# Two transformer blocks on one core: another order of projection items and of hosted weights, and TensorE products that nobody reads in the norms

## The reference, cut to what matters

```python
def first_block(x, c, ...):
    for l in range(2):
        sh1, sc1, g1, sh2, sc2, g2 = split(silu(c) @ w_ada[l] + b_ada[l])
        h = x * (1 + sc1) + sh1
        y = mixer(h)                       # h @ w_in, attention, @ w_o
        x = layer_norm(ALPHA * x + (1 + g1) * y)
        h = x * (1 + sc2) + sh2
        x = layer_norm(ALPHA * x + (1 + g2) * swiglu(h, w_ffn_in[l], w_ffn_out[l]))

def second_block(x, c, ctx, c_ctx, ...):
    for l in range(2):
        mod_x, mod_c = ada_params(c, w_ada[l]), ada_params(c_ctx, w_ada[l])   # 9 vectors each
        x, h_ctx = swiglu_half_step(x, mod_x), swiglu_half_step(h_ctx, mod_c)
        p = modulate(rms_norm(x)) @ w_in[l]          # q, k, v; rms norm and rotation per head
        x = x + gate * (attention(p) @ w_out[l])
        x, h_ctx = swiglu_half_step(x, mod_x), swiglu_half_step(h_ctx, mod_c)
```

## Time and profile before

| | |
|---|---|
| median of 3 runs | 2866.78 us (2857.04 to 2866.90) |
| profiled execution | 2865.56 us, its span 2863.7 us |
| mean granted TensorE clock | 0.937 |
| busy: TensorE, VectorE, ScalarE, GpSimd | 2611.6, 1771.5, 1083.2, 226.9 us |
| DMA | 413.74 MB, mean 144 GB/s |

### The profile page before, as it was taken

The page is one execution under the profiler, slowest core; times in us unless marked ns, Lnnn a source line. Parts: engine busy times, 40 slices in busy tenths (PEclk is TensorE's granted clock), DMA queues, the critical chain, the costliest instruction groups (busy, mean ns, idle before and its releaser), DMA issues.

```text
span 2863.7 us, 39671 instructions
## 1 busy us (share of the span) xinstructions
PE 2611.6 (91%) x15379; PEld 2228.5 (78%) x15379; DVE 1771.5 (62%) x3184; ACT 1083.2 (38%) x2068; POOL 226.9 (8%) x170
## 2 busy tenths in 40 slices
PE   4767998897997899998999899999899998999999
PEld 4746997867997688887875678888688887877899
DVE  6567776658776656546559675555565433568654
ACT  2343543444443333323338333322333322336553
POOL 2000100000100211101000021110111100100110
PEclk8868999979999999998899999999999999789999
DMA  8923775814765244332520334433344433441553
GB/s 291 279 96 118 265 247 165 263 50 148 240 224 184 78 143 133 131 125 90 152 74 2 118 103 144 135 125 114 100 147 132 133 121 128 105 128 61 178 186 122
DMA packets 354869, 413.74 MB, mean 144 GB/s; under 512 B 24737, under 2 KB 291914, under 8 KB 354618
## 3 DMA queue, kind: packets, MB, share of 16 engines
q1 hardware_dynamic: 352496, 404.13, 44.2%
q0 software_dynamic: 832, 4.65, 0.5%
q10 hardware_dynamic: 1354, 2.43, 0.2%
HBM read 409.56 MB, written 5.27 MB: 145 GB/s over the span
## 4 chain that ended last, share of the span: by engine, by line
PE 62%; DVE 9%; ACT 2%; DMA 2%; issue 1%; POOL 0%; DVEq 0%; ACTq 0%; POOLq 0%
PE bank L894 61%; DVE ada_partial L1533 2%; DMA raw_weights<-in_w_ffn_in_dram 2%; DVE H_hi L1660 1%; DVE weight_lo L682 1%; PE bank L1146 1%; DVE tmp L1643 1%; DVE rstd L1633 1%; ACT weight_hi L1230 1%; DVE X L1648 0%; DVE rstd L1755 0%; DVE bias L1759 0%; DVE X L1715 0%; POOL H_lo L852 0%; DVE bank L1795 0%
## 5 line engine op out<-in xcount | busy, mean ns | idle before, releaser
L682 DVE TENSOR_TENSOR weight_lo<-raw_weights,weight_hi 128x512 fp32r<-128x512 f32 x1024 | 776.1, 765 | 915.9 <-ACT weight_hi L1230 905.1
L1230 ACT ACTIVATE weight_hi<-raw_weights 128x512 fp32r<-128x512 f32 x1024 | 634.1, 629 | 1355.5 <-PE bank L894 1226.1
L894 PE MATMUL bank<-H_hi,weight_hi 128*128 128x256 f32 (+1 forms) x2832 | 973.7, 344 | 109.4 <-POOL H_lo L852 79.9
L894 PE MATMUL bank<-H_lo,weight_hi 128*128 128x256 f32 (+1 forms) x2832 | 955.0, 337 | 0.0
L894 PE MATMUL bank<-H_hi,weight_lo 128*128 128x256 f32 (+1 forms) x2832 | 953.9, 337 | 0.0
L894 PEld LDWEIGHTS bank<-H_hi,weight_hi 128*128 128x128 f32 x2832 | 554.4, 196 | 192.3 <-issue 119.2
L894 PEld LDWEIGHTS bank<-H_hi,weight_lo 128*128 128x128 f32 x2832 | 554.5, 196 | 52.0
L894 PEld LDWEIGHTS bank<-H_lo,weight_hi 128*128 128x128 f32 x2832 | 555.2, 196 | 49.0 <-issue 1.0
L1533 DVE SCALAR_TENSOR_TENSOR ada_partial<-raw_weights,silu_c,ada_partial 128x512 f32<-128x512 f32 x616 | 441.6, 744 | 1.6 <-issue 0.4
L894 PE MATMUL bank<-hidden_hi,weight_hi 128*128 128x256 f32 (+1 forms) x1056 | 358.3, 339 | 3.2 <-DVE weight_lo L682 3.2
L894 PE MATMUL bank<-hidden_hi,weight_lo 128*128 128x256 f32 (+1 forms) x1056 | 354.9, 336 | 0.0
(11 more groups left out here) (170 smaller groups left out, 2050.1 us busy)
## 6 DMA issues: line engine op xcount, KB each, us to landing
raw_weights<-in_w_ada_dram SPq DMA_DIRECT2D x120, 1024.0 KB, 5.3
raw_weights<-in_w_ffn_up_dram SPq DMA_DIRECT2D x88, 1024.0 KB, 5.3
raw_weights<-in_w_ffn_in_dram SPq DMA_DIRECT2D x44, 1024.0 KB, 6.0
raw_weights<-in_w_ffn_down_dram SPq DMA_DIRECT2D x32, 1024.0 KB, 5.1
raw_weights<-in_w_in_dram SPq DMA_DIRECT2D x18, 1024.0 KB, 6.0
raw_weights<-in_w_ffn_out_dram SPq DMA_DIRECT2D x16, 1024.0 KB, 7.7
raw_weights<-in_w_in_ab_dram SPq DMA_DIRECT2D x12, 1024.0 KB, 9.8
raw_weights<-in_w_in_cd_dram SPq DMA_DIRECT2D x12, 1024.0 KB, 8.7
```

Of the source, the lines that this page charges most:

```text
L682: eng.tensor_tensor(WL[:, p.g % SPLIT, 0:p.kt * CW].rearrange("p (t n) -> p t n", n=CW), raw_ap(ch.n, ch.kt, CW)[:, p.k0:p.k0 + p.kt, :], ...
L894: return pe.matmul(o, w, x, start=start, stop=stop, skip_group_check=True)
L1230: act.activation(WH[:, p.g % SPLIT, 0:p.kt * CW].rearrange("p (t n) -> p t n", n=CW), raw_ap(ch.n, ch.kt, CW)[:, p.k0:p.k0 + p.kt, :], ACT ...
```

## The change

- In layers 2 and 3 the `k 0` item comes before `kv`; the first round of the norm per head is renamed to match.
- The projection of layer 0 hosts 10 chunks instead of 12, that of layer 2 five instead of four, that of layer 3 two instead of four. The last `ffn_in`, which had no host, hosts what is left (three chunks, in its first three steps); the tests for a host are now made per step.
- TensorE gets `busy(n)`: n fp32 products of `ident` with `ones` into a PSUM bank that the stage does not use otherwise; nobody reads them. An `rms` norm has 6 before its wait for X and 22 behind its last sum; an `ln` norm 4 before, 4 behind the sums of X, one behind each square product, and 12 at the end.
- VectorE's steps of `ffn_in` are written out by one call; their order is the same.

```diff
-    ROUNDS = ((12, 8, 9), (10, 11, 4, 5), (6, 7, 0, 1), (2, 3))
+    ROUNDS = ((8, 9, 12), (10, 11, 4, 5), (6, 7, 0, 1), (2, 3))
...
-            a1 = ada_chunk() if host else None
+            a1 = ada_chunk() if host and len(ADA) < sum(ADA_CHUNKS) else None
...
+        done = len(ADA) if steps[-1].host is None and host else None
+        add("ffn_in", hosted=done, n=n, steps=steps, ...
...
-            groups.append(Rows(chunks=cs, host=ada_chunk() if host and m < 3 else None,
+            groups.append(Rows(chunks=cs, host=ada_chunk() if steps[-1].host and m < 3 else None,
...
-        all_hosted = len(ADA) if len(ADA) == sum(ADA_CHUNKS) else None
+        all_hosted = len(ADA) if ada == 3 else None
...
-         (2816, ("v", 768))], T, 12, T, 0)
+         (2816, ("v", 768))], T, 10, T, 0)
...
-            [(2048, ("kv",)), (1024, ("k", 0)), (1280, ("k", 2)), ...
-             (256, ("q", 2)), (1536, ("v", 0)), (1792, ("v", 256))], n, 4, T if last else n, 2 + l)
+            [(1024, ("k", 0)), (2048, ("kv",)), (1280, ("k", 2)), ...
+             (256, ("q", 2)), (1536, ("v", 0)), (1792, ("v", 256))], n, 2 if last else 5, T if last else n, 2 + l)
...
-        ffn(a["w_ffn_up_2"][l, 1], a["w_ffn_down_2"][l, 1], n2, 2 + l, 8, True, not last, False)
+        ffn(a["w_ffn_up_2"][l, 1], a["w_ffn_down_2"][l, 1], n2, 2 + l, 8, True, True, False)
...
+        def busy(n):
+            for _ in range(n):
+                mm(B_T[1][:, 0:P], ident[:, :], ones[:, :], True, True)
+
         def stats(s, before):
+            busy(6 if s.kind == "rms" else 4)
             pe.wait_ge(x_ready.sem, s.x)
             for m in range(3 if before.kind == "proj" else 0, 4):
                 sums(s, m)
             if s.kind == "ln":
+                busy(4)
                 for t in range(NT):
                     squares(s, t, B_T[0])
+                    busy(1)
+            busy(22 if s.kind == "rms" else 12)
...
+            if s.hosted:
+                close(s.hosted)
```

More of the change, by code:

```diff
@@ L519, in ffn @@
             g = chunk("g", view(w_in), 0, KC, CW * s)
-            a1 = ada_chunk() if host else None
+            a1 = ada_chunk() if host and len(ADA) < sum(ADA_CHUNKS) else None
             u = chunk("g", view(w_in), 0, KC, DFF + CW * s)
             steps.append(Step(g=g, u=u, host=a1, gg=group("act"), ug=group("dve")))
-        add("ffn_in", n=n, steps=steps, silu=silu_g.take(11), a32=act32.take(11), hi=act_hi.take(11),
+        done = len(ADA) if steps[-1].host is None and host else None
+        add("ffn_in", hosted=done, n=n, steps=steps, silu=silu_g.take(11), a32=act32.take(11), hi=act_hi.take(11),
             ready=act_ready.take(11), host=host)
@@ L641, in _build @@
         qkv(a["w_in_2"][l],
-            [(2048, ("kv",)), (1024, ("k", 0)), (1280, ("k", 2)), (512, ("q", 4)), (768, ("q", 6)), (0, ("q", 0)),
-             (256, ("q", 2)), (1536, ("v", 0)), (1792, ("v", 256))], n, 4, T if last else n, 2 + l)
+            [(1024, ("k", 0)), (2048, ("kv",)), (1280, ("k", 2)), (512, ("q", 4)), (768, ("q", 6)), (0, ("q", 0)),
+             (256, ("q", 2)), (1536, ("v", 0)), (1792, ("v", 256))], n, 2 if last else 5, T if last else n, 2 + l)
         add("bias", what="na", layer=l, take=bias_in.take(16 * 34))
@@ L742, in step @@
                 load(at, lambda k: s.steps[k].g)
-                if s.host:
+                if s.steps[at.u].host:
                     load(at, lambda k: s.steps[k].host)
@@ L1669, in step @@
             def step(at):
-                ahead_of(at, lambda k: s.steps[k].g, (lambda k: s.steps[k].host) if s.host else None)
+                ahead_of(at, lambda k: s.steps[k].g, (lambda k: s.steps[k].host) if s.steps[at.u].host else None)
                 ahead_of(at, lambda k: s.steps[k].u)
@@ L1681, in step @@
                 dve.sem_inc(ev_dve.sem, 1)
[L1682 to L1688, removed]
+            each(dve, 0, 11, 2, step)
+            if s.hosted:
+                close(s.hosted)
         def proj(s):
```

## The result

The changed kernel took 2820.7 us (median of four, 2814.8 to 2827.6) where the one before took 2865.5: ratio 0.9846, 95% interval 0.9821 to 0.9871. That is 44.8 us less. Run again beside other kernels (`after_again`) it took 2823.9 us (six, 2817.6 to 2838.8), ratio 0.9861 (0.9834 to 0.9887). The profiled execution is the longest of the first four: 2827.6 us, span 2825.8, which is 37.9 us under the span before. So the traces can account for 37.9 us; the other 7 are in how the changed kernel's executions differ among themselves, and they differ with the clock (0.964 at 2814.8 us, 0.963 and 0.962 at 2819.6 and 2821.9, 0.959 at 2827.6).

What follows compares the result with a forecast made beforehand. TensorE was taken as the bound, by its own stream, its stops and slices at half clock. Terms -12.1 - 10.6 - 6.3 - 2.6 + 1.9 - 4 = -33.7 us took 2865.6 to 2832 us; range 2822 to 2856.

Steps and rivals of the forecast that it cites:

- Part 1, layer 2: Layer 2 projection: with `k 0` before `kv`, first product to the item behind takes 35.8 us, not 47.9; 12.1 us less.
- The fifth host, put at 0: Layer 2 projection: a fifth hosted item, 8 more partial products on VectorE, hidden behind TensorE; 0, at worst 2 us.
- Part 1, layer 3: Layer 3 projection: the same reordering takes 35.0 us, not 45.6; 10.6 us less.
- the term put at 0: Layer 3 projection: losing two hosts changes nothing, since they hid behind TensorE; 0 us.
- Part 2: Layer 0 projection: two hosts fewer let scores start about 154.9 instead of 161.16; -6.3 us, bounds 0 and -7.
- Part 3: Moved hosted chunks: layer 1's first two feed-forward steps 12.2 us each, -2.6 us; two sums in the last feed-forward, +1.9 us.
- Part 4: Norms: unread products at 0.23 us each lie mostly in waits and warm the statistics; together -4.3, taken as -4 us.
- The one that I gave 0.21: Rival: `kv` falls back in layer 2 alone, behind its 16-instruction sum; -12.1 becomes about +2, 2846 us; chance 0.21.
- Unread products costing on the path: Rival: in the norms they cost +3.4 in each of four layer norms; 2852 us at most, 2845 middle; chance 0.09.
- both `kv` cold: Rival: `kv` is cold wherever it stands, layers 2 and 3 pay +4 and +5 instead of gaining; 2863 us; chance 0.12.
- the slower case: Rival: the clock counts neither fp32 unread nor narrow products; `kv` cold twice, unread ones cold too; 2883 us; chance 0.03.

Runs made afterwards that it cites:

- b_order: The kernel before with only `k 0` put ahead of `kv`, hosts as before and no unread products: 2841.2 us, ratio 0.9912.
- b_unread: The kernel before with only the unread products added, in all ten norms; `kv` first and hosts as before: 2859.0 us, ratio 0.9969.
- b_hosts: The kernel before with only the hosted chunks moved as in the change; `kv` first, no unread products: 2854.0 us, ratio 0.9947.
- a_no_unread: The changed kernel without its unread products, all else as changed: 2843.1 us, ratio 0.9916.
- a_shift9: The changed kernel with nine more unread products (2.1 us) between the halves of layer 2's first feed-forward: 2842.2 us, ratio 0.9907.
- a_shift4: The changed kernel with four more unread products (0.9 us) between the halves of layer 2's first feed-forward: 2828.5 us, ratio 0.9849.

## Why the prediction was off, point by point

**Part 1, layer 2: right.** `k 0` to its last tile is 15.04 us (15.06), the sum 1.70 (1.71), `kv` 16.35 instead of 17.5: a tile is 2.04, the narrow products (2.04 - 3 x 0.25)/12 = 0.108 apart, just beyond the lower bound of 0.11, and the 32-bit loads of the ada sum were a good guide. From the first product to the item behind, 1365.38 - 1330.80 = 34.6, so 13.3 less instead of 12.1. The Trainium skill (TensorE: Matmul & The Clock Gate, Back-to-back issue gap) gives about 81 ns for a 128-column product with its load, and an estimate from that had `kv` at 13.8 us; the trace, with 16.35, does not agree. The fifth host, put at 0, costs its sum: from there to the first scores 102.70 us after 101.15 (1490.66 - 1389.51, the first scores before), 1.6 more.

**Part 1, layer 3: the size was off.** -10.6 was forecast; from the first product to the first scores it is 2526.10 - 2413.15 = 112.95 after 128.74 (2565.66 - 2436.92), 15.8 less. The item pair gave 11.9, a sum that no longer stands on the path 0.8, and 3.1 came from what I had not costed: TensorE waits 1.99 us for a reciprocal in both kernels; before, the clock was at 0.53 for the 10.94 us behind that wait, after at 0.78 for 7.83 us with the same work. Part of this goes with the hosts that layer 3 lost, which I had put at 0. The same work behind that wait, over the same 45 or 46 products, in the kernel before, in `b_order` and `b_unread`, which have layer 3's four hosts as well, and in `b_hosts`, which has two:
```profile
2514.66:2526.03 11.37, 11.37 (x45) 8.76 (x46) 4.57 (x8) 1.44 (x3) 0.00 (x0) 0.55 0.63 200
2487.31:2497.11 9.80, 9.80 (x45) 7.93 (x46) 4.57 (x8) 1.43 (x3) 0.00 (x0) 0.65 0.75 237
2509.03:2517.36 8.33, 8.33 (x46) 6.42 (x46) 4.57 (x8) 1.44 (x3) 0.00 (x0) 0.80 0.89 279
2507.07:2513.88 6.81, 6.81 (x46) 5.34 (x46) 4.56 (x8) 1.44 (x3) 0.00 (x0) 1.00 0.49 156
```
So with four hosts it takes 8.3 to 11.4 us in three profiles; the fourteen with two show 6.8 us (eight of them) or 8.3 (six, the changed kernel among them). From the norm's reciprocal to attention `b_hosts` takes 133.8 us after 141.3, and `a_no_unread` 123.6 after `b_order`'s 128.3. By these pairs of single profiles, and the changed kernel's 125.1, the term put at 0 is worth 3 to 7.5 us, sums included, and it accounts for what `b_hosts` gave beyond the 7 expected. Why the clock is higher behind that wait with two hosts fewer, no run shows.

**Part 2: right.** Scores start at 154.59 (forecast 154.9), -6.6 us for the -6.3.

**Part 3.** The last feed-forward is 1.5 longer (1.9). Layer 1's stage gave less than 2.6: ada sums two steps apart come 26.0 and 26.5 us apart where they were 26.8 and 27.0, so 1.3 in all; its first item takes 0.7 of that back (13.77 us at 0.55 after 13.11 at 0.86). A step is still VectorE's, at 13.0 us and not 12.2.

**Part 4: this step failed.** I took the unread products at -4, counting the cover and the faster sums of squares, and nothing for what they do to the clock of the stages behind them. The local terms came out: 0.23 us each, over 2.76 us before the first tile, squares of `rms` no longer cold (-1.6 once, though `b_hosts` has the same 786.4 us without any unread product), 8 squares of a layer norm with their unread products in 5.1 us. What they are worth beside the new order and hosts is 20 to 23 us (2823.9 against 2846.7, and 2820.7 against 2843.1), on the kernel before 8.1, and with the sum moved behind `kv` 1.4 that is not clear of noise: there is no one price, and most of it is not local. Some 9 to 11 us of the 20 to 23 go with `kv` of layer 2, cold in part of the executions without them, 14 us each time: that is what taking the sum away without any unread product gave by the ratios. `kv` was not cold in the profile of any kernel with all of them and the hosts of the change, unless delayed by 2.1 us. Where the rest lies is not shown. Layer 0's feed-forward with its norm took 225.6 and 225.9 us in the two profiles without them, 221.2 and 225.0 in the two with them. Layer 1's attention with its output took 95.5 and 90.8 against 87.9 and 93.8, but over all profiles without unread products in attention it varies from 81.7 to 95.5, with them in the norms and without. The other side of the same mistake: order and hosts were put at -29.7 together and give 22 to 24 in this company. The two errors partly cancel, and that, by luck, is why the sum was only 11 us off.

**The rivals.** The one that I gave 0.21 names the right place, and its price was right too: with `kv` fallen the stage takes 163.8 us after 161.9, +1.9 for the +2. I held it for a matter of the kernel and it is one of each execution. Unread products costing on the path, and both `kv` cold, are refuted by the profile of the changed kernel, and so is the slower case: `kv` ran at 1.00 there, and so did the unread products but for the four ahead of the first layer norm's squares.

**What stays open.** Why the sum comes at a harmless moment in both profiled executions of the changed kernel and, by their times, in most of the other eight, when unread products in either part of the norms do not bring that about. The runs show only that one delay, in one place, brings the fall back. Some 10 of the 20 to 23 us that the unread products are worth have no place yet.

## What to carry to other kernels

A profile shows one execution. Where the clock's level depends on when a lull comes, read several executions, their spread and their mean clock, before you price an edit: a median 14 us off and a spread of 25 us can be one item that falls in some of them. A sum of one-column products directly ahead of narrow ones is a place to mend, but only the times of several executions tell what mending it gives: with the sum one item later, ahead of wide products, the kernel without unread products gained 9 to 11 us, and the one with them gained nothing: short falls made that stage 6.3 us longer (155.7 after 149.4). And parts of a change that touch the clock do not add up: time each alone and with the others in place. A term put at nothing is a term too: two hosts fewer in layer 3, put at 0, were worth 3 to 7.5 us.

## What was not expected of the hardware

- The same instructions, in the same program, ran at 1.00 in one execution and fell to 0.50 in another (16.35 and 29.37 us of `kv`), after 1.84 us of 16 one-column products; in the changed kernel a delay of 2.1 us far ahead of them brought the fall where one of 0.9 us had not (29.29 us of `kv` in `a_shift9`, 16.36 in `a_shift4`).
- An item of 128-column products that starts at the full level can hold it for 16 us with no gap, and can also lose it within its first tile; one that starts at the lower level stays there for 30.75 us, and was not lifted by 5.0 us of unread products at 1.00 that ended 2.76 us ahead of it.
- In attention, with two unread products in each wait, the clock was at the full level for all of 55 us (0.50 for 37 us in the changed kernel without them), and layer 1's attention and output took 79.6 us in both kernels that have them, where the others took 81.7 to 95.5.
